# Mixture-of-experts hidden blocks: four of seven chunks transposed in 32x32 blocks and by a trip through memory, and the first expert slots loaded at another time

## The reference, cut to what matters

```python
def swiglu(x, w13, w2):
    a, g = jnp.split(x @ w13, 2, axis=-1)
    return (jax.nn.silu(a) * g) @ w2

def moe_ffn(x, router_w, router_b, w13, w2):      # TOP_K = 2, N_EXPERTS = 8, D_FF_E = 3584
    ...
    for e in range(N_EXPERTS):
        y = y + gate[..., e:e + 1] * swiglu(x, w13[e], w2[e])
    return y
```

## Time and profile before

| | us |
|---|---|
| median of 3 runs | 2236.96 (2236.05 to 2237.69) |
| the profiled execution, its own time | 2238.39 |
| its span, first to last instruction | 2237.0 |
| TensorE busy | 2217.7 (99%) |
| VectorE busy | 1760.3 (79%) |
| ScalarE busy | 1364.5 (61%) |
| GpSimd busy | 167.5 (7%) |
| mean granted TensorE clock, of full speed | 0.998 |
| moved by DMA | 611.39 MB, mean 273 GB/s |

### The profile page before, as it was taken

One profiled execution on the slowest core, in us unless ns is written; L12 is line 12 of the kernel. 1 busy time (PEld: TensorE's weight loads), 2 busy tenths in 40 slices (PEclk: granted clock), 3 DMA queues, 4 the chain that ended last, 5 costly groups with the idle time before them and its releaser, 6 DMA issues.

```text
span 2237.0 us, 30263 instructions
## 1 busy us (share of the span) xinstructions
PE 2217.7 (99%) x12156; PEld 1904.7 (85%) x12156; DVE 1760.3 (79%) x2253; ACT 1364.5 (61%) x1764; POOL 167.5 (7%) x231
## 2 busy tenths in 40 slices
PE   9999999999999999999999999999999999999997
PEld 7998888998888999888899887888888888888886
DVE  7976656977564588665678898999999998989898
ACT  5654444655443454444455577777777777877775
POOL 3100111300120000211100010000000000000001
PEclk9999999999999999999999999999999999999999
DMA  8455764546763535776625699999999999999996
GB/s 279 151 191 212 240 233 154 176 170 215 246 235 132 185 132 208 245 236 205 226 93 187 249 349 406 386 380 388 376 382 382 386 370 386 373 392 360 390 372 251
DMA packets 104163, 611.39 MB, mean 273 GB/s; under 512 B 24056, under 2 KB 25384, under 8 KB 34896
## 3 DMA queue, kind: packets, MB, share of 16 engines
q1 hardware_dynamic: 80496, 568.76, 67.3%
q0 software_dynamic: 9872, 31.12, 4.0%
q10 hardware_dynamic: 13648, 9.50, 1.6%
HBM read 591.07 MB, written 18.62 MB: 273 GB/s over the span
## 4 chain that ended last, share of the span: by engine, by line
PE 96%; DVE 3%; DMA 1%; ACT 0%; issue 0%; SPq 0%; POOL 0%; DVEq 0%
PE bank L491 28%; PE bank L493 28%; PE bank L492 28%; PE bank L488 8%; DVE wl L1662 2%; PE bank L768 1%; PE bank L721 1%; PE bank L521 1%; DMA spare<-in_ws 1%; DMA raw<-in_ws 0%; PE bank L816 0%; PE bank L1088 0%; DVE TU L1873 0%; DVE EL L1689 0%; ACT wh L1189 0%
## 5 line engine op out<-in xcount | busy, mean ns | idle before, releaser
L1662 DVE TENSOR_TENSOR wl<-raw,wh 128x1024 fp32r<-128x1024 f32 x698 | 819.9, 1223 | 219.9 <-ACT wh L1189 216.7
L1189 ACT ACTIVATE wh<-raw 128x1024 fp32r<-128x1024 f32 x704 | 704.3, 1052 | 331.1 <-PE bank L493 295.2
L491 PE MATMUL bank<-wh,GH 128*128 128x512 f32 x896 | 352.8, 394 | 0.0
L493 PE MATMUL bank<-wh,GL 128*128 128x512 f32 x896 | 349.3, 390 | 0.0
L492 PE MATMUL bank<-wl,GH 128*128 128x512 f32 x896 | 348.8, 389 | 0.0
L1662 DVE TENSOR_TENSOR wl<-spare,wh 128x1024 fp32r<-128x1024 f32 x264 | 309.8, 1221 | 26.8 <-ACT wh L1189 25.3
L1189 ACT ACTIVATE wh<-spare 128x1024 fp32r<-128x1024 f32 x264 | 264.2, 1054 | 61.0 <-PE bank L493 56.9
L491 PE MATMUL bank<-HH,wh 128*128 128x256 f32 x832 | 239.6, 288 | 0.1
L492 PE MATMUL bank<-HL,wh 128*128 128x256 f32 x832 | 235.3, 283 | 0.0
L493 PE MATMUL bank<-HH,wl 128*128 128x256 f32 x832 | 235.2, 283 | 0.0
L491 PE MATMUL bank<-wh,HH 128*128 128x512 f32 (+1 forms) x600 | 223.4, 372 | 0.0
(11 more groups left out here) (319 smaller groups left out, 3537.1 us busy)
## 6 DMA issues: line engine op xcount, KB each, us to landing
raw<-in_ws SPq DMA_DIRECT2D x352, 1024.0 KB, 6.6
spare<-in_ws SPq DMA_DIRECT2D x132, 1024.0 KB, 7.1
more<-in_ws SPq DMA_DIRECT2D x48, 1024.0 KB, 5.0
scratch_blocks<-TB POOLq DMA_DIRECT2D x30, 256.0 KB, 2.9
TURNED<-scratch_blocks POOLq DMA_DIRECT2D x36, 128.0 KB, 4.8
once<-in_ws SPq DMA_DIRECT2D x4, 1024.0 KB, 11.4
scratch_parts<-Y POOLq DMA_DIRECT2D x7, 512.0 KB, 8.5
REL<-in_relb ACTq DMA_DIRECT2D x4, 768.0 KB, 13.3
```

The lines of the kernel that those rows point to most:

```text
L491: T.q.matmul(o, l[0], r[0], start=start, stop=False)
L493: return T.q.matmul(o, l[1], r[0], start=False, stop=stop)
L1189: A.q.activation(sets[c % NSET][0][:, half * i:half * i + half], raws[stream.place[n]][:, half * i:half * i + half], ACT.Copy).then_inc(*h ...
L1662: V.q.tensor_tensor(wl[:, half * i:half * i + half], raw[:, half * i:half * i + half], wh[:, half * i:half * i + half].bitcast(f32), ALU.s ...
```

## The change

In the first four of seven chunks of each expert (`E_BLOCKS = 4`), the hidden values are turned as in the dense layers: VectorE writes the product in the other order, transposes it in 32x32 blocks into TT1, GpSimd writes it to a DRAM scratch tensor in one DMA and reads it back in four into BIAS, and two chunks later ScalarE rounds it and VectorE takes the rest. The last three chunks stay with TensorE. VectorE now waits for the DRAM write of chunk c before the product of chunk c + 1. GpSimd's other work stands in its queue behind the blocks of the same expert. The single-use buffers become five; once0 lies in BIAS and is loaded once the last attention scores are read, once1 after the turned mixer rows, once2 and once3 after the output product, once4 after the last normalisation. The load of the last gain and bias goes from `a_router` to the end of expert 1. The helper functions that stay as they are (`turn`, `a_hi`, `v_lo`) are left out; the diff:

```diff
--- before.py
+++ after.py
@@ -13,6 +13,11 @@
 SLOT = 2048
 F_CHUNKS = [(512 * i, 512 * i + 512) for i in range(5)] + [(2560, 2816)]
 E_CHUNKS = [(512 * i, 512 * i + 512) for i in range(7)]
+E_BLOCKS = 4
+
+
+def by_blocks(i, c):
+    return isinstance(i, tuple) and i[1] < 8 and c < E_BLOCKS
 
 
 
@@ -265,7 +270,7 @@
             self.number.append(c)
             c += split
         ring = ["raw0", "raw1", "raw2"]
-        more, once, spare = ["more0", "more1"], ["once0", "once1", "once2", "once3"], ["spare0", "spare1"]
+        more, once, spare = ["more0", "more1"], [f"once{i}" for i in range(5)], ["spare0", "spare1"]
         into = {BASE[0] + MIX + 3: more, BASE[1] + MIX + 3: more, BASE[2] + BR + 3: more}
         self.place, self.before, self.turn = [], [], []
         held, turns = {}, {}
@@ -295,6 +300,7 @@
     sent = nc.dram_tensor("scratch_sent", (8 * 128, 1024), f32).ap()
     parts = nc.dram_tensor("scratch_parts", (7 * 128, 1024), f32).ap()
     blocks = nc.dram_tensor("scratch_blocks", (6, 2 * 128 * 512), f32).ap()
+    rows_blocks = nc.dram_tensor("scratch_hidden", (E_BLOCKS, 128 * 512), f32).ap()
     stream = Stream()
     ctx = ExitStack()
     with ctx:
@@ -358,8 +364,9 @@
         for i in range(2):
             raws[f"more{i}"] = at(f"more{i}", 16384 + 2048 * i, SLOT)
             raws[f"spare{i}"] = nc.alloc_sbuf_tensor_at(f"spare{i}", [128, SLOT], f32, offset=h_at + 4 * SLOT * i)
-        for i, a in enumerate((0, 2048, 4096, 14336)):
-            raws[f"once{i}"] = at(f"once{i}", a, SLOT)
+        raws["once0"] = nc.alloc_sbuf_tensor_at("once0", [128, SLOT], f32, offset=arena_at + 4 * 22016)
+        for i, a in enumerate((4096, 0, 2048, 14336)):
+            raws[f"once{i + 1}"] = at(f"once{i + 1}", a, SLOT)
         banks = [ctx.enter_context(nc.psum_tensor(f"bank{i}", [128, 512], f32)) for i in range(8)]
 
         ident = CST[:, C_ID:C_ID + 128]
@@ -474,6 +481,7 @@
         part_out = [signal(f"part{i}_out", 16) for i in range(2)]
         choice_in = [signal(f"choice{i}_in", 16) for i in range(4)]
         blocked, blocks_out, hidden_done = signal("blocked"), signal("blocks_out", 16), signal("hidden_done")
+        row_blocks_out, row_blocks_in = signal("row_blocks_out", 16), [signal(f"row_blocks{i}_in", 16) for i in range(2)]
         blocks_in = [signal(f"blocks{i}_in", 16) for i in range(2)]
         flag, select, selr, yhi, ydone = (signal(n) for n in ("flag", "select", "selr", "yhi", "ydone"))
         groups = Groups(banks, *([ctx.enter_context(nc.semaphore(f"s_{n}{i}")) for i in range(8)]
@@ -745,7 +753,7 @@
                 turn()
                 if between:
                     between.pop(0)()
-                if tiles == 1:
+                if tiles == 1 and not by_blocks(i, c):
                     left.append((c, 0, n))
             return turn
 
@@ -1153,8 +1161,9 @@
                     later[5] = past
                 ready = (lambda k, t: out("gt", e, k // 4)) if 2 <= e < 8 else (lambda k, t: out("ga", e // 2, 1, k // 2))
                 turn = t_swiglu(expert_slot(e), GV[e % 2], ready, E_CHUNKS, 1, ("e", e), between)
-                t_down(expert_slot(e) + 28, EV, lambda k, t: out("tu", ("e", e), k // 4, 0), 28, "dn", ("e", e), 1, turn,
-                       between=later)
+                t_down(expert_slot(e) + 28, EV, lambda k, t: (
+                    hidden_done.at(("e", e), k // 4) if by_blocks(("e", e), k // 4) else out("tu", ("e", e), k // 4, 0)),
+                       28, "dn", ("e", e), 1, turn, between=later)
             t_last_scatter(8 * page + 7)
 
         def t_warm():
@@ -1302,6 +1311,16 @@
             nf = (F_CHUNKS[c][1] - F_CHUNKS[c][0]) // 128
             src = TURNED[c % 2][:, 0:256 * nf].rearrange("p (b f q) -> p f b q", b=8, f=nf)
             return [src] + [v[:, 4 * c:4 * c + nf, :].rearrange("p f (b q) -> p f b q", b=8) for v in FV]
+
+        def row_parts(c):
+
+            src = BIAS[:, 2048 + 512 * (c % 2):2560 + 512 * (c % 2)].rearrange("p (b f q) -> p f b q", b=4, f=4)
+            return [src] + [v[:, 4 * c:4 * c + 4, :].rearrange("p f (b q) -> p f b q", b=4) for v in EV]
+
+        def a_row_blocks(i, c):
+            src, hi_part, _ = row_parts(c)
+            A.wait_ge(*row_blocks_in[c % 2].at(i, c, 3))
+            A.q.activation(hi_part, src, ACT.Copy, scale=1.0).then_inc(*part.mark("hidden", i, c))
 
         def a_hidden(l, c):
             src, hi_part, _ = turned_parts(c)
@@ -1347,6 +1366,8 @@
                 turn()
                 if tiles == 2 and c >= 2:
                     a_hidden(i, c - 2)
+                if c >= 2 and by_blocks(i, c - 2):
+                    a_row_blocks(i, c - 2)
                 if between:
                     between.pop(0)()
                 for t in range(tiles):
@@ -1536,9 +1557,6 @@
             a_turn_x(7, 1)
             tokens(1)
             A.wait_ge(*top.at(3, "c", 1))
-            A.q.dma_start(BIAS[:, 0:2048], bass.AP(ln_d.tensor, 3 * 2048, [[0, 128], [1, 2048]])
-                          ).then_inc(*ln_in.mark(8))
-
         def a_gates():
             for t in range(2):
                 A.wait_ge(*gap.at(t))
@@ -1596,6 +1614,10 @@
                         turn()
                     if 3 <= j < 3 + len(later):
                         later[j - 3]()
+                if e == 1:
+                    A.wait_ge(*lo_of(EXPERTS + 2).at(EXPERTS + 2, 1))
+                    A.q.dma_start(BIAS[:, 0:2048], bass.AP(ln_d.tensor, 3 * 2048, [[0, 128], [1, 2048]])
+                                  ).then_inc(*ln_in.mark(8))
                 if e < 7:
                     a_down_copy(e)
                     continue
@@ -1805,6 +1827,11 @@
             src, hi_part, lo_part = turned_parts(c)
             V.wait_ge(*part.at("hidden", l, c))
             V.q.tensor_tensor(lo_part, src, hi_part.bitcast(f32), ALU.subtract).then_inc(*hidden_done.mark(l, c))
+
+        def v_row_blocks(i, c):
+            src, hi_part, lo_part = row_parts(c)
+            V.wait_ge(*part.at("hidden", i, c))
+            V.q.tensor_tensor(lo_part, src, hi_part.bitcast(f32), ALU.subtract).then_inc(*hidden_done.mark(i, c))
 
         def v_blocks(l, c, t, n):
 
@@ -1854,6 +1881,8 @@
                 turn()
                 if tiles == 2 and c >= 2:
                     v_hidden(i, c - 2)
+                if c >= 2 and by_blocks(i, c - 2):
+                    v_row_blocks(i, c - 2)
                 if between:
                     between.pop(0)()
                 for t in range(tiles):
@@ -1868,8 +1897,19 @@
                                           ALU.mult).then_inc(*groups.empty("gu", i, c, t))
                         v_blocks(i, c, t, n)
                         continue
+                    if by_blocks(i, c):
+                        if c:
+                            V.wait_ge(*blocked.at(i, c - 1))
+                            V.wait_ge(*row_blocks_out.at(i, c - 1))
+                        gate, up = (v[:, 0:n].rearrange("p (f a r) -> p f a r", a=4, r=32)
+                                    for v in (TT[t], groups.bank("gu", i, c, t)))
+                        V.q.tensor_tensor(TU[t][:, 0:n].rearrange("p (a f r) -> p f a r", a=4, r=32), gate, up,
+                                          ALU.mult).then_inc(*groups.empty("gu", i, c, t))
+                        V.wait_ge(*out("gu", i, c, t))
+                        V.q.transpose(TT[1][:, 0:n], TU[t][:, 0:n]).then_inc(*blocked.mark(i, c))
+                        continue
                     if c:
-                        V.wait_ge(*full("tu", i, c - 1, t))
+                        V.wait_ge(*(blocked.at(i, c - 1) if by_blocks(i, c - 1) else full("tu", i, c - 1, t)))
                     V.q.tensor_tensor(TU[t][:, 0:n], TT[t][:, 0:n], groups.bank("gu", i, c, t)[:, 0:n],
                                       ALU.mult).then_inc(*groups.empty("gu", i, c, t))
                     left.append((c, t, n, c0 // 128))
@@ -2679,6 +2719,22 @@
                                   bass.AP(blocks.tensor, 131072 * c + n // 4 * a, [[n, 32], [32 * n, 8], [1, n // 4]])
                                   ).then_inc(*blocks_in[c % 2].mark(l, c, a))
 
+        def g_row_blocks(e):
+
+            for c in range(E_BLOCKS):
+                i = ("e", e)
+                G.wait_ge(*blocked.at(i, c))
+                G.q.dma_start(bass.AP(rows_blocks.tensor, 65536 * c, [[512, 128], [1, 512]]),
+                              TT[1][:, :]).then_inc(*row_blocks_out.mark(i, c))
+                G.wait_ge(*row_blocks_out.at(i, c))
+                if c >= 2:
+                    G.wait_ge(*hidden_done.at(i, c - 2))
+                for a in range(4):
+                    G.q.dma_start(BIAS[32 * a:32 * a + 32, 2048 + 512 * (c % 2):2560 + 512 * (c % 2)].rearrange(
+                        "p (b n) -> p b n", b=4), bass.AP(rows_blocks.tensor, 65536 * c + 128 * a,
+                                                          [[512, 32], [16384, 4], [1, 128]])
```

(14 more changed lines are left out.)

## The result

| | before | after | ratio, 95% interval |
|---|---|---|---|
| median, us | 2236.96 | 2243.71 (2240.44 to 2250.91, 7 runs) | 1.0033 (1.0021 to 1.0045) |
| profiled execution, own time (span) | 2238.39 (2237.0) | 2240.44 (2239.2) | |

A forecast was written before the change was run, and what follows sets the result against it. TensorE was taken to bound the kernel, with 96% of the chain of work. The terms -13.6 + 1.1 + 0.9 + 1.0 = -10.6 us gave 2226.4 us at the median; own range 2222 to 2231 (0.52), whole range 2219 to 2241.

The forecast's parts named there:

- The transposes that go: TensorE, four groups an expert at 0.485 us: 15.5 us over 8 experts, 13.6 us of it on the path.
- VectorE: Block chunks: 32x32 transposes add 2.8 us an expert, hidden with 1 us of cover, except in the first expert.
- the +1.1: First expert: TensorE stalls 3.0 us on VectorE's added work, against 1.94 us saved on transposes.
- the +0.9 of the first expert: First expert, where scatter and blocks meet: 0.9 us more wait for weights than the 2.31 before.
- The early fetch: First expert slots loaded before the normalisation's end, with one buffer more: nothing gained; bounds 0 and 2.3 us won.
- The new waits: VectorE waits for a block's write, ScalarE for its read-back two chunks on: hidden, likely 18 us against 21.8.
- the cover: VectorE's wait before product c+1: 10.5 us for the block's write to land, taken as 6.
- Rival (c): Block writes land too late, VectorE waits and TensorE runs dry: 2262 us at 12 us landing; chance 0.11.
- DMA: Block trips of 2.1 MB an expert: 405 GB/s needed, 428 reached; 0.15 us lost an expert, 1 us in all.
- The nearest row: Two 0.5 MB transfers at 1514 us, 323 and 316 GB/s for ten us, used to price small transfers.
- a lead of 4: Weight loads' lead of at least 4 us, against a deficit of 2 to 5, regained in the down product.
- rival (b): DMA volume takes the gain back, 1 to 1.7 us lost an expert: 2236 to 2240 us; chance 0.18.

The follow-up runs named there:

- the whole kernel with the store in pieces: Changed kernel, but four DMAs store 32 partitions each in 512-byte pieces, putting blocks in place, and one DMA reads 128 rows back: 2225.68 us, ratio 0.9945.
- the five-chunk version: Five block chunks instead of four, against the kernel whose store puts the blocks in place: 2227.75 us, ratio 0.9951 to the kernel before the change.

## Why the prediction was wrong

**The transposes that go: right.** 0.485 us a group. Where nothing else intervenes the stretches are 117.63 us, and 115.74 in the whole kernel with the store in pieces; forecast were 117.7 and 115.7.

**VectorE: right in size; its net effect doesn't show.** The products of the first expert in the changed kernel, VectorE and TensorE in order of time, answer to the earlier trace rows:

```profile
1285.22 0.69 DVE L1906 TENSOR_TENSOR TU<-TT,bank 128x512 f32<-128x512 f32 x1 [0.46 <-ACT TT L1377]
1285.95 0.71 DVE L1909 STREAM_TRANSPOSE TT<-TU 128x512 f32<-128x512 f32 x1
...
1333.78 0.69 DVE L1913 TENSOR_TENSOR TU<-TT,bank 128x512 f32<-128x512 f32 x1
```

```profile
1324.05 0.47 PE L499 MATMUL bank<-wh,GH 128*128 128x512 f32 x1 [0.80 <-DVE wl L1684]
...
1335.74 0.47 PE L499 MATMUL bank<-wh,GH 128*128 128x512 f32 x1 [0.53 <-DVE wl L1684]
```

48.6 us from the first product to the fifth, the forecast to the tenth, and TensorE then waits for low parts: 2.3 us from 1272 to 1356, where it waited for nothing before and 3.0 were forecast. The last turn should have come 1 to 3 us later and comes 0.8 earlier (1356.41); the wait just before it, kept in the forecast, shrank from 2.31 to 0.38 us. In single traces of the other runs this turn lies between 1355.6 and 1358.5, so neither the +1.1 nor the +0.9 of the first expert can be confirmed. In later experts VectorE did hide its work: without the trip nobody waited.

**The early fetch: right**, nothing (ratio 1.0001).

**The new waits: right that they hide.** Issues of 1360 to 2187 us, count, KB and median us to landing:

```profile
scratch_hidden<-TT POOLq DMA_DIRECT2D x28, 256.0 KB, 7.1
BIAS<-scratch_hidden POOLq DMA_DIRECT2D x112, 64.0 KB, 6.3
```

The store lands in 7.1 us where the cover was 10.5, and the trace has no wait of VectorE for it. Rival (c) is out.

**DMA: the step that failed.** The prediction put it so: "What small transfers cost beyond their bytes is unknown", bounded it by a store and a row load at 1514 us, 2.5 to 4 us per MB, and took 0.15 us lost an expert, 1 us in all, with 0.9 for the first expert. Measured are 14.8 us over seven experts in the profiled execution, and 18.0 in all by the medians. The price failed in two ways.

The nearest row was misread. In the ten us at 323 and 316 GB/s (1510 to 1520) GpSimd's queue moved only 0.26 MB of its 1.05, and nothing before 1515; 0.75 MB moved in the next five, at 428 GB/s. So most of the slow time passed while the side transfers moved little or nothing, and these rows are no price for them. What made the ten us slow stays open.

And it had the wrong shape. The store and the row load cover all 128 partitions, and such trips are free here: by their bytes they need 2.1 / 0.4245 = 4.9 us an expert. The change's reads fill 32 partitions each and cost 1.0 us a trip more, 4.0 an expert: 8.9 us, 4.3 per MB, above the prediction's bounds. Put into its own sum, this gives a deficit of 39.2 + 1.3 + 8.9 - 43.5 = 5.9 us against a lead of 4, an estimate of 1.9 us lost an expert; 2.1 are measured. (The fit is in part luck, since the lead of 4 came from the misread rows.)

It came out as rival (b), which had 0.18, in mechanism (lead used up, ScalarE behind late slots), though not for DMA volume or small size. Its price of 2236 to 2240 was too low by 4 to 8 us: it let 1 to 1.7 us go an expert where 2.1 went in the fastest execution, and the median is 3.3 us above that one. The 3 to 5 us that it had for the first expert don't show.

What could have told: the Trainium skill, "SBUF — State Buffer", section "Door 1: The DMA port swizzle", says that a DMA reaches only 8 of the 16 ports of SBUF when it covers 32 partitions, and no more when it covers 64. The runs agree for transfers that fill SBUF: quarters and halves cost alike (2243.7 and 2242.3 us), full ones nothing. For quarter transfers that leave SBUF the runs show no cost (2225.7 us). By that rule alone, a read of 0.26 MB at half the rate would hold the DMA an estimated 0.6 us longer; measured is 1.0.

**What stays open.** Why the five-chunk version gains nothing is not shown. Its longer waits for weights point at the DMA: block chunks need 434 GB/s by the prediction's sum and get 424, and there is one more of them to an expert. Nor is it shown why quarter stores are free where quarter reads are not, or what a read into, say, 96 partitions would cost.

## What to carry to other kernels

When a kernel's weights keep the DMA engines nearly full, the shape of a small side transfer counts more than its bytes: let every DMA that fills SBUF cover all 128 partitions, and put a rearrangement into the store, where it was free. Price a new transfer by a row with the same number of partitions and the same direction, not only by one of like size. And beside the mean rate work out how far the loads may run ahead over the busiest few chunks: two more buffers took back the same 18 us with the dear reads left in.

## What the hardware did that was not expected

- Reads from DRAM into 32 or 64 partitions beside full-rate loads lower the total from 424 to between 381 and 390 GB/s, with the DMA engines shown busy all the time (share 1.01 and 1.02).
- Pieces of 512 bytes were as good as rows of 2 KB (2224.99 and 2224.90 us), and four DMAs as good as one (2226.08).
- The kernels that waited long for weights spread more: 2240 to 2251 us for the changed one (7 runs), 2224.5 to 2226.0 for the one with the store in pieces (4 runs).
